# A hybrid layer on one Trainium2 core: the mixer's first loads, four fewer early units, and the routing stage's order

## The chip, the cores and the metric

The kernel runs on one core of one Trainium2 chip. The metric is device time in microseconds for one execution of the whole program, as the median of repeated runs. The engines are TensorE (PE, matmuls, with its weight loads shown as PEld), VectorE (DVE), ScalarE (ACT), GpSimd (POOL) and SyncE (SP, which here only issues DMAs). Each runs its own instruction stream in order, and they meet at semaphores.

## What is computed

One decoder layer on 2048 tokens of width 1024, all in float32:

```python
u = x*(1+scale1) + shift1                      # scale, shift, gates: silu(c) @ w_ada + b_ada
cb, cc, cx, q, k, v, ga, gb = split(u @ w_in)
y_a = (cb * causal_dwconv3(cc*cx)) @ w_a
y_b = stick_breaking_attention(q, k, v) @ w_b  # 8 heads of 64, no softmax
mix = (sigmoid(ga)*y_a + sigmoid(gb)*y_b) @ w_o
x = layer_norm(alpha*x + g1*mix)
u2 = x*(1+scale2) + shift2
# router: aff = sigmoid(u2 @ w_router); best group of 4 by its two best experts,
# top 2 of 16 experts inside it, gates normalized
x = layer_norm(alpha*x + g2*moe(u2))           # each expert: (silu(u@w_gate) * (u@w_up)) @ w_down
```

Float32 precision is reached with pairs: an operand is split into a rounded high part (`hi`, made by an ACT copy) and the rest (`lo`, a subtraction on DVE or POOL), and a product is three matmuls: hi*hi, hi*lo and lo*hi (`product`, line 92).

## The kernel before

The program is a row of stages. A stage is a block: every engine has a stream in it, and the next block begins on all engines when all streams of the last have ended.

**front** makes the first modulation rows, u and the projection to q, k and v, in 4 token blocks of 12 units each (48 units, `n` in the loops). A unit's result is evicted by ACT (hi, line 354) and DVE (lo, lines 412 and 416) into one of two stages and stored by SP (lines 226 to 231). Besides, front makes "halves": for a column block of `w_in` that the mixer needs, it loads 0.5 MB, splits it and stores hi and lo (1 MB) to DRAM. `FRONT_FILL` (line 436) is how many of them, 18, one at every second unit from 10 on (`FILL_AT`; load at line 210, store at line 216). At unit 36 SP also reloads u, 4 MB (line 246).

**mixer** has 8 heads of 16 query tiles (t = 0 to 15). For each tile: scores for two tiles ahead on PE (`scores`, lines 738 to 741), two sigmoids on ACT (851, 852), a scan on DVE (907), a product on POOL (700, `weigh`), transposes on PE (752), hi on ACT (870) and lo on DVE (915), then values on PE (771, 773). Between these PE fills in the projection to the convolution and gate columns: 14 units per head, 8 contraction steps each, cut over the slots by `fill_plan`. Units 0 to 13 belong to head 0, 14 to 27 to head 1; they are one token block, and later token blocks use the same 28 halves again. Unit n below 18 takes its halves from DRAM (`load_halves`, 553). Units 18 to 27 load the raw block (561), split it on ACT (843) and POOL (693), and SP keeps the result in DRAM (543). Scores need key block 0 (`k0`) for t below 4 and the rest of the keys (`k`, 1.5 MB, lines 575 and 582) from the second bank of t = 4 on, which PE works on in step t = 2. After each even tile DVE adds a modulation piece (`add_mod`, 964 and 967), 64 pieces of 0.25 MB in all; PE sums a head's pieces at its end (line 806). `k0` of head 0 is loaded through ACT's queue (835). SP's list starts with q, halves 0, q, v0, halves 1, k, mod 0, mod 1, v (lines 624 to 632).

**branch_outputs** makes the merged branches. **mix_norm_route** then does, for each of 16 token tiles t: `mix(t)`, 48 matmuls in 8 portions of 6 (PE, two PSUM buffers); `norm` on DVE (1519 to 1525); reciprocal deviation on POOL (1459 to 1463); the normalization on ACT (1402); `affine` on DVE (1531, 1533), which gives u2; scaling of x1 on POOL (1472, 1474); on PE the turn of u2 of tile t-2 (1300) inside step t; its copy out of PSUM on ACT (`rows_out`, 1381), then the logits on PE (1312) and a sigmoid on ACT (1390). ACT's order in step t is `rows_out(t-2)`, normalization of t, `high(t+3)`, `affinities(t-2)`. Tiles are grouped in sets; for a set DVE runs `choose` and `weigh` (1547 to 1589, some 27 small operations), PE ranks (1322, 1323), DVE runs `put` (1598 to 1603), and POOL scatters the records (1446, two per tile). At the end DVE makes the table of blocks (1624 to 1643). During this stage SP also loads expert 0's weights.

**experts** then reads the record of block 0 (POOL, 1709), gathers its rows (1719), turns them (PE, 1762), splits expert 0's gate and up weights (ACT 1829, DVE 1883, eight chunks each), and runs the blocks. **final_norm** ends it.

The order around the change is written out by hand:

```python
SETS = ((0, 4), (4, 8), (8, 12), (12, 14), (14, 16))
CHOOSE_AT = {5: 0, 9: 1, 13: 2, 16: 3, 17: 4}   # DVE step: set
RANK_AT = {7: 0, 11: 1, 15: 2, 17: 3, 18: 4}    # PE step: set (DVE's put too)
```

Of the kernel before, what the change touches and what calls it, by code (L numbers as in the profile page):

```python
# [435 lines left out]
FRONT_FILL = 18  # L436
# [18 lines left out]
def mixer(nc, used, keep, w_in, w_ada, u, u_in, u_saved, qk_hi, qk_lo, v_tok, halves, conv_t, gate_t, o_t, mod_rows):  # L455
# [49 lines left out]
    with ExitStack() as ctx:  # L505
# [32 lines left out]
        def _(sp):  # L538
# [91 lines left out]
            load_mod(0)  # L630
# [548 lines left out]
def mix_norm_route(nc, used, keep, stay, ahead, w_gate, w_up, w_down, m_t, x, mod_rows, ln1_g, ln1_b, w_router, b_router, acc, u2_rows, records):  # L1179
# [3 lines left out]
    SETS = ((0, 4), (4, 8), (8, 12), (12, 14), (14, 16))  # L1183
# [4 lines left out]
    CHOOSE_AT = {5: 0, 9: 1, 13: 2, 16: 3, 17: 4}  # L1188
    RANK_AT = {7: 0, 11: 1, 15: 2, 17: 3, 18: 4}
    with ExitStack() as ctx:  # L1190
        s = Scope(nc, ctx, "mix", used)
# [5 lines left out]
        y, x1t = s.sb("y", [P, D]), s.sb("x1t", [P, 2, D])  # L1197
# [88 lines left out]
        def _(pe):  # L1286
# [70 lines left out]
        def _(act):  # L1357
# [35 lines left out]
            for t in range(STEPS):  # L1393
# [20 lines left out]
        def _(pool):
# [34 lines left out]
            def scatter_at(step):  # L1449
                for at_step, g in RANK_AT.items():  # L1450
                    for t in range(*SETS[g]):
                        if step == min(at_step + 1 + t - SETS[g][0], max(at_step + 1, NT)):
                            scatter(t)

            for t in range(NT + 4):
                if t < NT:
                    past(pool, m["normed"], t)
                    pool.wait_ge(m["var_done"], t + 1)
                    pool.tensor_scalar(var[:], mv[:, 1:2], EPS, None, ALU.add).then_inc(m["var_step"], 1)
                    pool.wait_ge(m["var_step"], 2 * t + 1)  # L1460
                    pool.tensor_tensor(rstd[:], var[:], minus_half[:], ALU.pow).then_inc(m["var_step"], 1)
                    pool.wait_ge(m["var_step"], 2 * t + 2)
                    pool.tensor_scalar(offset[:], mv[:, 0:1], rstd[:], -1.0, ALU.mult, ALU.mult
                                       ).then_inc(m["rstd_done"], 1)
# [633 lines left out]
```

## Time and profile before

| What | Value |
|---|---|
| Median of 3 runs | 2816.57 us (2816.51 to 2819.57) |
| Profiled execution | 2813.91 us |
| Its span, first to last instruction | 2812.3 us |
| PE / DVE / ACT / POOL busy | 2507.2 / 1479.4 / 1114.9 / 816.4 us |
| Granted TensorE clock, mean | 0.949 |
| Halves loads in the mixer | 102 pairs of 512 KB |

The profile's page gives each engine's busy share in 40 slices. Views of the trace used below are the windows (busy time of each engine in a stretch, and PEclk, the granted share of full clock: 1.00 is 2.4 GHz and 0.50 is 1.2 GHz), the timeline (start, duration, engine, line, instruction and, in brackets, how long the engine had been idle before it and what released it), and the list of DMA issues with the median time to landing.

### The profile page before, as it was taken

What the parts mean: (1) busy time and instruction counts of PE and PEld (TensorE: products, weight loads), DVE (VectorE), ACT (ScalarE), POOL (GpSimd) and SP (SyncE); (2) the same over time, 40 slices, a digit from 0 to 9 for tenths busy, and PEclk for the clock granted to TensorE, in tenths of its full rate; (3) what the DMA queues carried; (4) which work ended last, traced back from release to release, by engine and by line L of the source; (5) the groups of instructions that cost most, each with busy time, mean ns of one, the idle gap of its engine ahead of it and who ended that gap; (6) DMA issues with size and microseconds to landing.
All of it is one profiled execution on the core that took longest, in us unless ns stands there. A gap on an engine that the chain in (4) does not pass through costs nothing. (4 is left out here: it accounts for less than half of the span.)

```text
span 2812.3 us, 36346 instructions
## 1 busy us (share of the span) xinstructions
PE 2507.2 (89%) x12521; PEld 2092.3 (74%) x12522; DVE 1479.4 (53%) x1898; ACT 1114.9 (40%) x1814; POOL 816.4 (29%) x703
## 2 busy tenths in 40 slices
PE   5999789999999999999968969983998999999970
PEld 4788578878888888888857758773887888888750
DVE  6122156666566656566632256765446544526636
ACT  2122244545454545454520012112456545536633
POOL 2111022442222222222301235456222222223236
PEclk9999899999999999999989989995999999999985
DMA  7699966766757574746456646423467655636735
GB/s 265 243 317 311 308 201 193 245 207 214 220 174 216 177 232 159 214 152 199 146 185 221 175 152 230 144 98 120 136 185 237 206 145 175 208 89 208 255 75 239
DMA packets 259931, 553.75 MB, mean 197 GB/s; under 512 B 23989, under 2 KB 93737, under 8 KB 259177
## 3 DMA queue, kind: packets, MB, share of 16 engines
q1 hardware_dynamic: 236904, 486.74, 52.4%
q0 software_dynamic: 15248, 46.62, 7.6%
q10 hardware_dynamic: 7664, 18.88, 1.7%
q8 instruction: 70, 1.15, 0.2%
q14 instruction: 45, 0.36, 0.0%
HBM read 399.14 MB, written 153.02 MB: 196 GB/s over the span
## 5 line engine op out<-in xcount | busy, mean ns | idle before, releaser
L92 PE MATMUL mx_acc<-u_u,mx_w_hi 128*128 128x512 f32 x1792 | 569.5, 399 | 0.9 <-DMA mx_w_lo<-halves 0.6
L700 POOL TENSOR_TENSOR mx_wt<-mx_wt,mx_rest 128x127 f32<-128x127 f32 (+15 forms) x128 | 271.5, 2121 | 764.7 <-DVE mx_rest L907 764.7
L92 PEld LDWEIGHTS mx_acc<-u_u,mx_w_hi 128*128 128x128 f32 x1792 | 325.0, 189 | 65.5 <-DMA mx_w_lo<-halves 1.9
L915 DVE TENSOR_TENSOR mx_wt_lo<-mx_p_t,mx_wt_hi 128x512 fp32r<-128x512 f32 (+2 forms) x320 | 192.3, 605 | 317.4 <-ACT mx_wt_hi L870 315.6
L92 PE MATMUL mx_acc<-u_u,mx_w_lo 128*128 128x512 f32 x896 | 351.7, 393 | 0.0
L870 ACT ACTIVATE mx_wt_hi<-mx_p_t 128x512 fp32r<-128x512 f32 (+2 forms) x320 | 171.0, 534 | 415.8 <-PE mx_p_t L752 358.5
L907 DVE TENSOR_TENSOR_SCAN mx_rest<-mx_rest,mx_zero 128x128 f32<-128x128 f32 (+15 forms) x128 | 312.1, 2438 | 11.4 <-ACT mx_wt L852 11.4
L92 PE MATMUL moe_p_gu<-moe_gu_hi,moe_x_hi 128*128 128x512 f32 x656 | 262.3, 400 | 15.1 <-DVE moe_gu_lo L1883 13.0
L92 PE MATMUL moe_p_gu<-moe_gu_hi,moe_x_lo 128*128 128x512 f32 x656 | 258.2, 394 | 0.0
L92 PE MATMUL moe_p_gu<-moe_gu_lo,moe_x_hi 128*128 128x512 f32 x656 | 258.0, 393 | 0.0
L851 ACT ACTIVATE mx_rest<-mx_p_z 128x512 f32<-128x512 f32 (+2 forms) x320 | 171.0, 534 | 96.3 <-PE mx_p_z L739 59.3
L92 PEld LDWEIGHTS mx_acc<-u_u,mx_w_lo 128*128 128x128 f32 x896 | 169.1, 189 | 38.5
L752 PE MATMUL mx_p_t<-keep_ident,mx_wt 128*128 128x128 f32 x1088 | 174.6, 276 | 25.8 <-POOL mx_wt L700 19.2
L752 PEld LDWEIGHTS mx_p_t<-keep_ident,mx_wt 128*128 128x128 f32 x1088 | 134.1, 141 | 80.9 <-POOL mx_wt L700 36.0
L852 ACT ACTIVATE mx_wt<-mx_p_z 128x512 f32<-128x512 f32 (+2 forms) x320 | 171.7, 536 | 0.0
L92 PE MATMUL fr_acc<-u_u,fr_w_hi 128*128 128x512 f32 x512 | 162.3, 399 | 6.5 <-DVE fr_stage L412 6.3
L1883 DVE TENSOR_TENSOR moe_gu_lo<-keep_stay,moe_gu_hi 128x1024 fp32r<-128x1024 f32 x128 | 146.8, 1219 | 28.4 <-ACT moe_gu_hi L1829 28.4
L1927 DVE TENSOR_TENSOR moe_h<-moe_p_gu,moe_act_g 128x256 f32<-128x256 f32 x82 | 31.0, 420 | 237.3 <-ACT moe_act_g L1860 237.3
L92 PEld LDWEIGHTS moe_p_gu<-moe_gu_hi,moe_x_hi 128*128 128x128 f32 x656 | 124.8, 190 | 41.2 <-DVE moe_gu_lo L1883 13.7
L738 PE MATMUL mx_p_z<-mx_k_hi,mx_q 128*128 128x512 f32 (+2 forms) x320 | 131.2, 410 | 19.4 <-DMA mx_k_lo<-qk_lo 19.4
L92 PEld LDWEIGHTS moe_p_gu<-moe_gu_hi,moe_x_lo 128*128 128x128 f32 x656 | 124.8, 190 | 27.1
L92 PEld LDWEIGHTS moe_p_gu<-moe_gu_lo,moe_x_hi 128*128 128x128 f32 x656 | 124.8, 190 | 25.2
(244 smaller groups left out, 5160.6 us busy)
## 6 DMA issues: line engine op xcount, KB each, us to landing
mx_w_hi<-halves SPq DMA_DIRECT2D x102, 512.0 KB, 3.9
mx_w_lo<-halves SPq DMA_DIRECT2D x102, 512.0 KB, 5.2
keep_stay<-in_w_gate SPq DMA_DIRECT2D x64, 512.0 KB, 4.3
keep_stay<-in_w_up SPq DMA_DIRECT2D x64, 512.0 KB, 5.2
keep_stay<-in_w_down SPq DMA_DIRECT2D x32, 1024.0 KB, 6.8
halves<-fr_ring SPq DMA_DIRECT2D x36, 512.0 KB, 6.5
u_saved<-u_u SPq DMA_DIRECT2D x4, 4096.0 KB, 19.5
mx_w_mod<-in_w_ada SPq DMA_DIRECT2D x64, 256.0 KB, 5.1
```

The lines of the kernel that those rows point to most:

```text
L92: mm = pe.matmul(out, a, b, start=first and n == 0, stop=last and n == len(pairs) - 1, skip_group_check=True)
L700: pool.tensor_tensor(wt[:, t % 2, 0:w - 1], wt[:, t % 2, 0:w - 1], rest[:, t % 2, 1:w], ALU.mult).then_inc(m["weights_done"], 1)
L738: pe.matmul(out, q, hi, start=True, stop=False, skip_group_check=True)
L752: mm = pe.transpose(p_t[:, n % TR, (j - 4 * r) * P:(j - 4 * r + 1) * P], wt[:, t % 2, j * P:(j + 1) * P], ident[:])
L851: act.activation(rest[:, t % 2, a:b], p_z[:, n % ZB, 0:b - a], ACT.Sigmoid, scale=-SCALE)
L852: act.activation(wt[:, t % 2, a:b], p_z[:, n % ZB, 0:b - a], ACT.Sigmoid, scale=SCALE).then_inc(m["z_used"], 1)
L870: act.activation(to, p_t[:, n % TR, 0:(k - j) * P].rearrange("p (j t) -> p j t", t=P), ACT.Copy).then_inc(m["hi_done"], 1)
L907: dve.tensor_tensor_scan(x[:, ::-1], x[:, ::-1], zero[:].to_broadcast([P, w]), 1.0, ALU.mult, ALU.max).then_inc(m["scan_done"], 1)
L915: dve.tensor_tensor(wt_lo[:, first:first + k - j], p_t[:, n % TR, 0:(k - j) * P].rearrange("p (j t) -> p j t", t=P), f32(wt_hi[:, first:fi ...
L1883: dve.tensor_tensor(lo, raw, f32(hi), ALU.subtract).then_inc(m["gu_lo_done"], 1)
L1927: dve.tensor_tensor(h[:, w], p_gu[:, 1, w], act_g[:, w], ALU.mult).then_inc(m["h_done"], 1)
```

## The change

- `FRONT_FILL` goes from 18 to 14. Front makes halves for head 0 only, and the mixer splits units 14 to 27.
- In the mixer `k0` of head 0 is issued by SP, first in its list; modulation piece 0 becomes fourth in the list (after `k0`, q and halves 0).
- Routing: the set (14, 16) becomes two sets of one tile; choices, ranks and puts get new steps, with `put` in a table of its own; PE turns after portion 0, ranks after portion 2 and does the logits after portion 3; ACT does `affinities(14)` after the normalization of 15; POOL's scatters are written out by step, some behind the x1 work.
- The table's last matmul uses the other half of the PSUM tile, and waits for the affinities.
- The first block's record and gather move from the experts stage to the end of the routing stage, on POOL. `y` of the routing stage and `x_raw` of the experts are one tile.
- `w_hi`, `w_lo` of the routing stage and `gu_hi`, `gu_lo` of the experts are one pair of tiles ("wide"). ACT makes all eight high chunks of expert 0 at the end of routing, DVE four low chunks; in the experts stage DVE makes two, then the low part of x, then the last two.
- In the experts stage PE turns x before its twelve transposes of zeros, POOL's memsets of the down weights come after gather 1, and SP waits for the first gather before it loads expert 1.

```diff
-FRONT_FILL = 18
+FRONT_FILL = UNITS_HEAD
@@ mixer, sync
+            load_k0(0)
             load_q(0)
             load_halves(0)
+            load_mod(0)
             load_q(1)
             load_v0(0)
             load_halves(1)
             load_k(0)
-            load_mod(0)
             load_mod(1)
@@ mixer, scalar
-            for half in range(2):
-                rows = slice(half * HD, (half + 1) * HD)
-                for dst, src in ((k0_hi, qk_hi), (k0_lo, qk_lo)):
-                    act.dma_start(f32(dst[rows, 0]), src[AW:AW + HD, 0:NB]).then_inc(k0_in[0], 16)
@@ mix_norm_route
-    SETS = ((0, 4), (4, 8), (8, 12), (12, 14), (14, 16))
+    SETS = ((0, 4), (4, 8), (8, 12), (12, 14), (14, 15), (15, 16))
-    CHOOSE_AT = {5: 0, 9: 1, 13: 2, 16: 3, 17: 4}
-    RANK_AT = {7: 0, 11: 1, 15: 2, 17: 3, 18: 4}
+    CHOOSE_AT = {5: 0, 9: 1, 13: 2, 14: 3, 15: 4, 16: 5}
+    RANK_AT = {7: 0, 11: 1, 15: 2, 16: 3, 17: 4, 18: 5}
+    PLACE_AT = {7: 0, 11: 1, 14: 2, 15: 3, 16: 4, 17: 5}
+    SCATTER_AT = {8: (0,), 9: (1,), 10: (2,), 11: (3,), 12: (4, 5), 13: (6, 7), 15: (10, 11)}
+    SCATTER_LATE = {14: (8, 9), 15: (12, 13, 14, 15)}
@@ mix_norm_route, tensor
-                        if k == 1:
+                        if k == 0:
                             turn(t - 2)
-                        if k == 5:
+                        if k == 2 and t in RANK_AT:
+                            rank(RANK_AT[t])
+                        if k == 3:
                             logits(t - 2)
-                        if k == 5 and t in RANK_AT:
-                            rank(RANK_AT[t])
...
-            pe.wait_ge(m["rank_used"], len(SETS))
-            pe.matmul(p_r[:, 1, 0:E], ones[:], seen[:, NT], start=True, stop=True).then_inc(m["ranked"], 1)
+            pe.wait_ge(m["aff_done"], len(SETS))
+            pe.matmul(p_r[:, 0, 0:E], ones[:], seen[:, NT], start=True, stop=True).then_inc(m["ranked"], 1)
@@ mix_norm_route, scalar
+                if t == NT - 1:
+                    affinities(NT - 2)
...
+            act.wait_ge(m["mix_done"], NT)
+            for k in range(KD):
+                if k % PIECE == 0:
+                    act.wait_ge(ahead["piece"][k // PIECE], 32)
+                act.activation(w_hi[:, k], gu_raw[:, k], ACT.Copy).then_inc(m["gu_hi_done"], 1)
@@ mix_norm_route, gpsimd
+            pool.wait_ge(m["row_set"], 1)
+            start = pool.value_load(block_row[0:1, 0:1], min_val=0, max_val=E * CAP)
+            pool.wait_ge(m["record_set"], 1)
             pool.wait_ge(m["scattered"], 32 * NT)
+            pool.dma_start(record[:, 4], records[bass.ds(start, P), :]).then_inc(ahead["record_in"], 16)
+            for i in range(UR):
+                pool.wait_ge(u2_stored[i], 16 * len(range(i, NT, UR)))
+            pool.wait_ge(m["normed"], NT)
+            pool.wait_ge(ahead["record_in"], 16)
+            pool.indirect_dma_start(out=first["x_raw"][:], out_offset=None, in_=u2_rows,
+                                    in_offset=bass.IndirectOffsetOnAxis(ap=record[:, 4, 0:1], axis=0)
+                                    ).then_inc(ahead["x_in"], 16)
@@ mix_norm_route, vector
+            for k in range(LO_AHEAD):        # LO_AHEAD = 4
+                dve.wait_ge(m["gu_hi_done"], k + 1)
+                dve.tensor_tensor(w_lo[:, k], gu_raw[:, k], f32(w_hi[:, k]), ALU.subtract).then_inc(m["gu_lo_done"], 1)
@@ experts
 sync:    +            sp.wait_ge(m["x_in"], 16)
 gpsimd:  -            load_record(0)
          -            gather_x(0)
 tensor:  +            turn_x(0)      (before the transposes of zeros, was behind them)
 vector:  -            split_gu(0, None)
          +            split_gu(0, 0, range(LO_AHEAD, LO_AHEAD + 2))
                       low_x(0)
          +            split_gu(0, 0, range(LO_AHEAD + 2, KD))
```

## Rows read from the trace of the kernel before

**Rows 1.** Windows: busy us (x) of PE, PEld, DVE, ACT, POOL; PEclk; DMA; GB/s

```profile
1890.00:1960.00 70.00, 27.82 (x126) 23.91 (x124) 41.24 (x117) 13.70 (x18) 39.95 (x36) 0.61 0.24 84
```

**Rows 2.** Timeline, front's end: start, us, engine, line, instruction [idle before <-releaser]

```profile
326.12 0.39 PE L92 MATMUL fr_acc<-fr_w_hi,u_u 128*128 128x512 f32 x1
...
329.57 0.60 ACT L354 ACTIVATE fr_stage<-fr_acc 128x512 fp32r<-128x512 f32 x1 [2.30 <-DMA v_tok<-fr_stage]
```

**Rows 3.** Timeline of PE and DVE, the mixer's start

```profile
345.89 0.44 PE L738 MATMUL mx_p_z<-mx_k_hi,mx_q 128*128 128x128 f32 x1 [19.38 <-DMA mx_k_lo<-qk_lo]
...
360.74 0.49 DVE L964 TENSOR_SCALAR mx_m_sum<-mx_w_mod,keep_csilu 128x512 f32<-128x512 f32 x1 [10.70 <-DMA mx_w_mod<-in_w_ada]
...
363.42 0.90 PE L752 MATMUL mx_p_t<-keep_ident,mx_wt 128*128 128x128 f32 x3 [6.69 <-POOL mx_wt L700]
...
366.36 1.16 PE L92 MATMUL mx_acc<-u_u,mx_w_hi 128*128 128x512 f32 x2
```

**Rows 4.** DMA issues, 335 to 375 us: KB each, median us to landing

```profile
mx_k_lo<-qk_lo SPq DMA_DIRECT2D x2, 384.0 KB, 13.1
```

**Rows 5.** Timeline of PE, line 806: ends of heads 0, 1, 2

```profile
490.93 1.00 PE L806 MATMUL mx_p_o<-keep_one,mx_m_sum 128*128 128x1 f32 x8
...
626.73 1.00 PE L806 MATMUL mx_p_o<-keep_one,mx_m_sum 128*128 128x1 f32 x8
...
758.97 1.00 PE L806 MATMUL mx_p_o<-keep_one,mx_m_sum 128*128 128x1 f32 x8
```

**Rows 6.** Timeline of PE, ACT and DVE, a regular routing step

```profile
1796.36 1.03 PE L1300 MATMUL mix_p_t<-keep_ident,mix_u 128*128 128x128 f32 x8
...
1800.10 1.06 ACT L1381 ACTIVATE mix_u2t<-mix_p_t 128x512 f32<-128x512 f32 x2
...
1802.69 1.85 PE L1312 MATMUL mix_p_r<-mix_wr,mix_u2t 128*128 128x16 f32 x16
...
1809.98 1.03 PE L1300 MATMUL mix_p_t<-keep_ident,mix_u 128*128 128x128 f32 x8
...
1807.46 1.28 DVE L1519 SCALAR_TENSOR_TENSOR mix_y<-keep_stay,mix_p_mix 128x512 f32<-128x512 f32 x2 [2.38 <-PE mix_p_mix L92]
```

**Rows 7.** Timeline of PE and DVE, routing step 11, behind a choice

```profile
1836.08 3.59 PE L1312 MATMUL mix_p_r<-mix_wr,mix_u2t 128*128 128x16 f32 x16 [5.99 <-ACT mix_u2t L1381]
...
1844.34 0.40 PE L92 MATMUL mix_p_mix<-mix_w_hi,mix_a_hi 128*128 128x512 f32 x1
...
1845.23 1.28 DVE L1519 SCALAR_TENSOR_TENSOR mix_y<-keep_stay,mix_p_mix 128x512 f32<-128x512 f32 x2 [5.31 <-PE mix_p_mix L92]
```

**Rows 8.** Timeline of POOL and DVE, the routing stage's end

```profile
1902.79 2.37 POOL L1474 TENSOR_TENSOR mix_x1t<-mix_x1t,mix_ln_b 128x1024 f32<-128x1024 f32 x1
...
1907.47 1.28 DVE L1519 SCALAR_TENSOR_TENSOR mix_y<-keep_stay,mix_p_mix 128x512 f32<-128x512 f32 x2 [6.96 <-PE mix_p_mix L92]
...
1917.78 2.42 DVE L1549 TENSOR_TENSOR mix_pairs<-mix_sel 128x128 f32<-128x128 f32 x1
...
1926.92 0.18 DVE L1547 TENSOR_TENSOR mix_sel<-mix_aff,mix_br 128x32 f32<-128x32 f32 x1
...
1933.66 0.22 DVE L1598 TENSOR_TENSOR mix_picked<-mix_chosen,mix_p_r 128x64 f32<-128x64 f32 x1 [0.24 <-issue]
...
1943.37 0.20 DVE L1643 CAST keep_block_row<-mix_p_t 1x54 int32<-1x54 f32 x1 [0.46 <-PE mix_p_t L1354]
```

**Rows 9.** Timeline of POOL and PE, the first expert block

```profile
1947.11 0.11 POOL L1723 MEMSET moe_record<- 128x10 uint32 x1 [6.92 <-POOLq L1190]
...
1967.27 0.79 PE L92 MATMUL moe_p_gu<-moe_gu_hi,moe_x_hi 128*128 128x512 f32 x1 [2.09 <-DVE moe_x_lo L1917]
```

**Rows 10.** Timeline of PE, routing step 2

```profile
1694.98 1.93 PE L1312 MATMUL mix_p_r<-mix_wr,mix_u2t 128*128 128x16 f32 x16 [2.67 <-ACT mix_u2t L1381]
```

**Rows 11.** DMA issues of the whole run, POOL's loads

```profile
moe_record<-records POOLq DMA_DIRECT2D x46, 1.0 KB, 3.1
moe_x_raw<-u_rows,moe_record POOLq DMA_INDIRECT x45, 5.1
```

More of the change, by code:

```diff
@@ L1447, in scatter @@
                                             ).then_inc(m["scattered"], 16)
[L1449 to L1464, printed above, removed]
+            pool.memset(record[:], 0).then_inc(m["record_set"], 1)
+            for t in range(NT):
+                past(pool, m["normed"], t)
+                pool.wait_ge(m["var_done"], t + 1)
+                pool.tensor_scalar(var[:], mv[:, 1:2], EPS, None, ALU.add).then_inc(m["var_step"], 1)
+                pool.wait_ge(m["var_step"], 2 * t + 1)
+                pool.tensor_tensor(rstd[:], var[:], minus_half[:], ALU.pow).then_inc(m["var_step"], 1)
+                pool.wait_ge(m["var_step"], 2 * t + 2)
+                pool.tensor_scalar(offset[:], mv[:, 0:1], rstd[:], -1.0, ALU.mult, ALU.mult
+                                   ).then_inc(m["rstd_done"], 1)
                 if t == 0:
@@ L1651, in experts @@
         gu_raw, dn_raw = expert_raw(stay)
-        gu_hi, gu_lo = s.sb("gu_hi", [P, KD, 2, FF], F32R), s.sb("gu_lo", [P, KD, 2, FF], F32R)
+        gu_hi, gu_lo = (w[:].rearrange("p k (g f) -> p k g f", g=2) for w in wide)
         dn_hi, dn_lo = s.sb("dn_hi", [P, KF, D], F32R), s.sb("dn_lo", [P, KF, D], F32R)
-        x_raw = s.sb("x_raw", [P, D])
+        x_raw, record = first["x_raw"], first["record"]
         x_hi, x_lo = s.sb("x_hi", [P, KD, P], F32R), s.sb("x_lo", [P, KD, P], F32R)
@@ L1875, in _, with split_gu @@
             dve.sem_inc(m["y_free"], 3)
+            dve.sem_inc(m["gu_lo_done"], LO_AHEAD)
             dve.sem_inc(m["dn_lo_done"], KF)
-            def split_gu(e, done):
-                for c in range(KD):
+            def split_gu(e, done, chunks=range(KD)):
+                for c in chunks:
                     raw, hi, lo = chunk(c)
@@ L2055, in hybrid_layer @@
             "table": s.sb("table", [P, 4, E], I32), "block_row": s.sb("block_row", [P, ROWS], I32),
-            "csilu": s.sb("csilu", [P, KD]), "one": s.sb("one", [P, 1]), "spare": s.sb("spare", [P, 24]),
+            "csilu": s.sb("csilu", [P, KD]), "one": s.sb("one", [P, 1]), "spare": s.sb("spare", [P, 8]),
+            "record": s.sb("record", [P, 5, 2], U32),
             "marks": {n: s.sem(f"mark_{n}") for n in ("sp", "act", "pool", "pe", "dve")},
         }
-        ahead = {"w_o": [s.sem(f"w_o{k}") for k in range(KD)], "piece": [s.sem(f"piece{i}") for i in range(PIECES)]}
+        ahead = {"w_o": [s.sem(f"w_o{k}") for k in range(KD)], "piece": [s.sem(f"piece{i}") for i in range(PIECES)],
+                 "record_in": s.sem("record_in"), "x_in": s.sem("x_in")}
         with ExitStack() as uctx:
@@ L2069, in hybrid_layer @@
         branch_outputs(nc, used, keep, stay, ahead, conv_t, o_t, gate_t, w_a, w_b, w_o, m_t)
-        mix_norm_route(nc, used, keep, stay, ahead, w_gate, w_up, w_down, m_t, x, mod_rows, ln1_g, ln1_b, w_router, b_router,
+        wide = tuple(s.sb(n, [P, KD, D], F32R) for n in ("wide_hi", "wide_lo"))
+        first = {"record": keep["record"], "x_raw": s.sb("x_raw", [P, D])}
+        mix_norm_route(nc, used, keep, stay, ahead, wide, first, w_gate, w_up, w_down, m_t, x, mod_rows, ln1_g, ln1_b, w_router, b_router,
                        acc, u2_rows, records)
@@ L2074, in hybrid_layer @@
             ln_g, ln_b = ls.sb("g", [P, D]), ls.sb("b", [P, D])
-            experts(nc, used, keep, stay, ahead, w_gate, w_up, w_down, mod_rows, ln2_g, ln2_b, u2_rows, records, acc, ln_g, ln_b)
+            experts(nc, used, keep, stay, ahead, wide, first, w_gate, w_up, w_down, mod_rows, ln2_g, ln2_b, u2_rows, records, acc, ln_g, ln_b)
             final_norm(nc, used, acc, ln_g, ln_b, out)
```

63 lines of the change are left out of this document (33 added, 30 removed).

## The prediction

> **What bounds the kernel now.** I read the windows by stage first. TensorE (PE) is nearly always busy, except where two stages meet and in the routing stage; in the 70 us at that stage's end it is busy for 27.8 at a granted clock of 0.61 [rows 1]. So a change pays only where it shortens a PE gap, and it costs wherever PE is made to wait. Next I read the timeline of the three places that the diff touches, with the idle time in brackets.
>
> Front into mixer: PE's last matmul starts at 326.12, but the last eviction of its results waits for an older store and starts at 329.57 [rows 2]. The mixer's first matmul comes at 345.89, after 19.4 us. Ten us later VectorE (DVE) stands 10.7 us for modulation piece 0, then PE stands 6.7 us for weights that come out of DVE and GpSimd (POOL) [rows 3].
>
> Routing: in a regular step PE turns tile t-2 after two of the eight portions and does its logits after six; ScalarE (ACT) finishes the copy that the logits need at 1801.16, 1.5 us ahead of PE [rows 6]. Where DVE chooses experts, that copy is late, since it sits on ACT behind the next tile's normalization, and PE stands 6 us [rows 7]. After the last mix DVE is the bound: normalization, two choices, the table [rows 8]. Then comes the gather of the first block [rows 9].
>
> **Part 1, front tail: -3.0 us.** The last four fills (halves made at units 38 to 44) go. Each was a 0.5 MB load and a 1 MB store on SP's queue. With that queue light the last eviction can start when PE ends (326.5) and not at 329.57: -3.0 [rows 2]. Ends: 0 if the u reload alone fills the queue, -5 if the last store lands sooner too.
>
> **Part 2, mixer start: -5 us.** Key block 0, q, halves 0 and modulation piece 0 are now in front. The 10.7 us wait for the piece, and PE's 6.7 behind it, vanish. What is late next is the rest of k, which the scores of t = 4 need right after the turn of t = 2. It is issued in this window with a median of 13.1 us to landing [rows 4], the last one 10 us after the mixer's start, so it is there at about 358.5, and 1.2 us later now that 0.26 MB of the piece goes ahead of it. Old PE passed that point at 365.8, just before the fill at 366.36 [rows 3]; new PE would, on the old clock face, at 359.7: -6.1. PE then still has waited some 5 us, so its clock is low for a few us as it is now, which takes 1 back. Ends: -3 (k later), -9.5 (k in time: 6.7 of wait and 3 of low clock saved).
>
> The key loads move from ACT's queue to SP's, past q, halves and v: 4 issues, 2.4 us later for all behind them. The Trainium skill (DMA: Bandwidth & Descriptors, "Issuing engines are not separate DMA queues") says that transfers of all engines interleave on the same 16 DMA engines and that a second issuer saves only issue time. By it this move costs 2.4 us of issue and wins no bandwidth, and the 3 us by which the first matmul might come earlier are not won in the end, since k still decides; this agrees with how I took it.
>
> **Part 3, four more units split in head 1: +1.5 us.** Head 1, with ten such units, lasts 135.8 us, head 2 with none 132.2 [rows 5]: 0.36 us each, so 1.4, and a little for units 14 to 17, which fall on short steps where POOL's 2.4 us subtraction stands before the next weights. Ends: 0 and +4.
>
> **Part 4, logits after the fourth portion, turn after the first: +14.9 us.** A portion is about 1.36 us (13.62 us from turn to turn, less turn and logits, over eight) [rows 6]. New turn: one portion earlier, 1795.0 on the row's clock; logits reached 0.9 + 3 x 1.36 later, at 1800.0. The copy is ready at 1801.16, because it waits on ACT behind the normalization of t-1, which hangs on the end of mix(t-1) and not on the turn. So PE waits 1.1 us where it waited for nothing. DVE waits 2.4 us for the mix of such a step [rows 6], so it isn't the bound and the step gets longer by all of it. Steps 3, 4, 5, 8, 9, 12 and 13: 7 x 1.1 = 7.7. Steps 6, 10 and 14 lie ahead of a choice that decides anyway. In steps 7 and 11 PE resumes at the same time as before, but with 24 matmuls to go instead of 12 and the rank already done. The clock stays low to 1844.3 [rows 7]: from the end of the logits at 1839.6 that is 11 matmuls of 0.43, then 13 of 0.23 (a portion's 1.36 over six), so 1847.3 and not 1845.2: +2.1 and, where the low clock lasts longer, +2.4; together 4.4. Step 2 waits for its logits as well: 12 matmuls more behind the wait, +2.8. Ends for all: +5 (no wait in regular steps) and +27 (each wait brings low clock).
>
> **Part 5, the last sets and the handover: -5.2 us.** Three choices of (12,13), 14 and 15 replace two. The first now runs before norm(15): DVE is held by POOL's x1 work to 1905.2, choice and gates take 6, so norm(15) starts at 1911.3 and not 1907.47: +3.8 [rows 8]. After that DVE has two choices as before, 6.7 us each from 1926.92 to 1933.66 [rows 8], once with POOL's two 2.5 us operations in its way as before; POOL's scatters of 10 and 11 only shift them. Table ready: 1947.6 instead of 1943.57, +4.0. Handover, before: 1943.57 to the first expert matmul at 1967.27 is 23.7, of it 3.5 to the next block's first instruction [rows 9]. After: 1.2 to read the row, 3.1 for the record (median to landing), 1.3 to issue the gather [rows 11], then the same 3.5, x there by then (5.1 from issue), turn 2.0 and the twelve zero transposes 3.0, now behind the turn: about 14.5, so -9.2. The weight splits, 9 us of DVE, hide behind it. Net -5.2; ends -9 and +2. The memsets of the down weights (7.1 us of POOL) are now behind gather 1 and end about when PE wants them, 13 us after its first matmul.
>
> That POOL holds DVE is read from a 0.29 us operation that took 2.42 [rows 8]. The Trainium skill (GPSIMD Engine Reference, Specifications) says that POOL shares its SBUF interface with VectorE and contends with VectorE instructions in a two-port mode or with two SBUF inputs. By it choice 14 is held for the 5 us of x1(15); if it were not, the sum would be 4.6 lower.
>
> **Sum:** -3.0 - 5.0 + 1.5 + 14.9 - 5.2 = +3.2. The profiled execution is 2813.91 (span 2812.3), so 2817.1; it lies 2.7 below the median of 2816.57, to which I add the same: 2819.8.
>
> **Rivals.**
> - A, the fourth portion costs nothing: copies are there, or the DVE backlog swallows the waits. For it: the first steps' waits hang on DVE. Against: the copy's end is 4.8 us behind the old turn in each regular step. Then 14.9 falls away: -11.7, 2805. Chance 0.12.
> - B, each new 1.1 us wait also brings low clock, on the slow side. Place: the regular routing steps. Step 2's wait of 2.7 us before the logits at 1694.98 had a short stretch of low clock behind it [rows 10]. Nine matmuls at 0.43 instead of 0.23 are 1.8; 1.8 x 7 = +12.6, so +15.8, 2832. It decides from where PE's share of a step is too small to hold the clock. Against: 1.1 is less than half of that wait, and PE is busy for 13.6 of 14.7 us. Chance 0.12.
> - C, the handover gives nothing: DVE's extra 4 us grow, as the scatters push POOL's x1 into the choices, and gather and block end queue up. Price +5.2: +8.4, 2825. Chance 0.12.
> - D, k comes in time, and the whole wait and low clock in head 0 go: -4.5 more, -1.3, 2815. Chance 0.14.
> - My forecast: 0.50, by itself 2815 to 2826.
>
> **How the numbers follow.** A measurement tells 0.2%, 5.6 us, from no change. Faster: A and a little of D, 0.14. Slower: B, most of C, and a fifth of my own case, 0.33. Same: 0.53. The range leaves out half of A and half of B: 2807 to 2832.
>
> **What would show it.** Right: the first mixer matmul some 5 to 7 us earlier; DVE without the wait for the piece and PE waiting for k instead; a bracket of about 1.1 us before the logits in regular routing steps, with 14.7 us from turn to turn; the table about 19 us later than before relative to the stage's start; some 14.5 us from table to first expert matmul. Wrong if regular steps still last 13.6, if k is no wait, or if the handover stays near 24.

## The result and the profile after the change

| | before | after |
|---|---|---|
| Median | 2816.57 us | 2830.55 us (2829.43 to 2843.11) |
| Ratio to before | | 1.0056, 95% interval 1.0042 to 1.0070 |
| Profiled execution, its span | 2813.91, 2812.3 us | 2829.43, 2826.7 us |
| Granted TensorE clock, mean | 0.949 | 0.948 |

The change makes the kernel slower by 0.56%, some 16 us. The forecast was 2819.8 us and no change; the time lies at the upper end of its range, where rival B stood (2832).

I compared the two traces at marks that both have. Times are from each kernel's own start; "first mix" is PE's first `mix_p_mix` matmul, "norm of 14" is DVE's first operation on the mix of tile 14, and "table" is DVE's cast of the block row.

| Mark or stretch | before | after | difference | forecast |
|---|---|---|---|---|
| First mixer matmul | 345.89 | 336.46 | -9.4 | -6 |
| End of head 0 | 490.93 | 480.11 | -10.8 | -8.0 |
| Head 1 | 135.80 | 140.24 | +4.4 | +1.5 |
| End of the mixer's last head | 1417.35 | 1411.08 | -6.3 | -6.5 |
| Mixer's end to first mix | 233.17 | 235.29 | +2.1 | 0 |
| First mix to norm of tile 14 | 242.06 | 266.46 | +24.4 | +14.9 |
| Norm of 14 to norm of 15 | 14.89 | 18.77 | +3.9 | +3.8 |
| Norm of 15 to table | 35.90 | 29.83 | -6.1 | +0.2 |
| Table to first expert matmul | 23.90 | 16.13 | -7.8 | -9.2 |
| First expert matmul to the end | 845.0 | 849.1 | +4.1 | 0 |

The stretch between mixer and first mix is untouched code; in the other kernels below it lasted between 229.9 and 236.7 us with no pattern, so its 2.1 us are scatter. The mixer's start scatters too: in the five kernels here with the old front and the old load order the first mixer matmul comes at 343.7 to 347.2 us and head 0 ends at 488.1 to 493.4, so differences to the one trace of before are good to some 3 us there.

**The mixer's start.** This timeline of after (start, duration, engine, line, instruction, and in brackets the idle time before it and its releaser) answers to [rows 2, 3].

```profile
324.02 0.39 PE L93 MATMUL fr_acc<-fr_w_hi,u_u 128*128 128x512 f32 x1
324.45 0.60 ACT L355 ACTIVATE fr_stage<-fr_acc 128x512 fp32r<-128x512 f32 x1 [4.84 <-PE fr_acc L93]
336.46 0.44 PE L740 MATMUL mx_p_z<-mx_k_hi,mx_q 128*128 128x128 f32 x1 [12.04 <-DMA mx_q<-qk_lo]
352.95 0.47 PE L740 MATMUL mx_p_z<-mx_k_hi,mx_q 128*128 128x128 f32 x1 [4.66 <-DMA mx_k_lo<-qk_lo]
353.47 0.75 DVE L964 SCALAR_TENSOR_TENSOR mx_m_sum<-mx_w_mod,keep_csilu,mx_m_sum 128x512 f32<-128x512 f32 x1 [2.48 <-DMA mx_w_mod<-in_w_ada]
```

The last eviction now waits for PE and not for a store. PE's 6.7 us behind DVE's wait are gone; the rest of k is late next, for 4.66 us, and DVE waits 2.5 us for a later piece, off the path.

**Head 1.** PE's timeline, its head ends and two waits in between that before hadn't (its longest in these tiles was 0.86 us).

```profile
480.11 1.00 PE L808 MATMUL mx_p_o<-keep_one,mx_m_sum 128*128 128x1 f32 x8
485.59 0.44 PE L754 MATMUL mx_p_t<-keep_ident,mx_wt 128*128 128x128 f32 x2 [1.78 <-POOL mx_wt L702]
508.01 0.65 PE L754 MATMUL mx_p_t<-keep_ident,mx_wt 128*128 128x128 f32 x4 [2.64 <-POOL mx_wt L702]
620.35 1.00 PE L808 MATMUL mx_p_o<-keep_one,mx_m_sum 128*128 128x1 f32 x8
```

POOL splits the weights of units 14 to 17 there, and its product for the attention comes late: 4.4 us for both waits, about what head 1 lost.

**Routing.** Two regular steps of after against [rows 6]: the logits with their wait, some of the matmuls behind them, the next turn.

```profile
1739.34 1.96 PE L1314 MATMUL mix_p_r<-mix_wr,mix_u2t 128*128 128x16 f32 x16 [1.09 <-ACT mix_u2t L1383]
...
1741.94 0.45 PE L93 MATMUL mix_p_mix<-keep_wide_hi,mix_a_hi 128*128 128x512 f32 x1
1742.19 0.63 PE L93 MATMUL mix_p_mix<-keep_wide_lo,mix_a_hi 128*128 128x512 f32 x1
1742.62 0.63 PE L93 MATMUL mix_p_mix<-keep_wide_hi,mix_a_lo 128*128 128x512 f32 x1
1743.04 0.63 PE L93 MATMUL mix_p_mix<-keep_wide_hi,mix_a_hi 128*128 128x512 f32 x1
...
1745.18 0.57 PE L93 MATMUL mix_p_mix<-keep_wide_hi,mix_a_lo 128*128 128x512 f32 x1
1745.59 0.39 PE L93 MATMUL mix_p_mix<-keep_wide_hi,mix_a_hi 128*128 128x512 f32 x1
...
1790.26 1.03 PE L1302 MATMUL mix_p_t<-keep_ident,mix_u 128*128 128x128 f32 x8
1793.26 1.24 ACT L1404 ACTIVATE mix_x1t<-keep_x_raw,mix_offset,mix_rstd 128x1024 f32<-128x1024 f32 x1 [16.19 <-POOL mix_offset L1466]
1795.36 1.06 ACT L1383 ACTIVATE mix_u2t<-mix_p_t 128x512 f32<-128x512 f32 x2
1796.47 1.96 PE L1314 MATMUL mix_p_r<-mix_wr,mix_u2t 128*128 128x16 f32 x16 [1.09 <-ACT mix_u2t L1383]
1798.28 0.49 PE L93 MATMUL mix_p_mix<-keep_wide_hi,mix_a_hi 128*128 128x512 f32 x1
...
1805.23 1.03 PE L1302 MATMUL mix_p_t<-keep_ident,mix_u 128*128 128x128 f32 x8
```

The wait is the forecast's, 1.09 us, and for its reason: the turn ends at 1791.3 and the copy starts at 1795.36, behind the normalization. Behind the second wait the matmuls go on at 0.23 us and the step lasts 14.97 us. Behind the first they fall to 0.43 us (the lower of the clock's two levels, 1.2 GHz) for eight matmuls, and that step lasts 16.6. Of the seven regular steps three lose 1.3 us against the 13.6 of before, and four lose 2.95.

**The end of routing and the first blocks**, against [rows 8, 9].

```profile
1912.83 1.28 DVE L1535 SCALAR_TENSOR_TENSOR keep_x_raw<-keep_stay,mix_p_mix 128x512 f32<-128x512 f32 x2
1931.60 1.28 DVE L1535 SCALAR_TENSOR_TENSOR keep_x_raw<-keep_stay,mix_p_mix 128x512 f32<-128x512 f32 x2
1959.42 0.96 POOL L1455 DMA_INDIRECT records<-mix_meta,mix_dest  x1 [0.30 <-issue]
1961.43 0.20 DVE L1659 CAST keep_block_row<-mix_p_t 1x54 int32<-1x54 f32 x1 [0.46 <-PE mix_p_t L1356]
1963.41 0.60 POOL L1484 DMA_DIRECT2D keep_record<-records  x1 [3.04 <-DMA records<-mix_meta,mix_dest]
1966.28 1.02 POOL L1489 DMA_INDIRECT keep_x_raw<-u_rows,keep_record  x1 [2.27 <-DMA keep_record<-records]
1972.59 1.94 PE L1779 MATMUL moe_p_x<-keep_ident,keep_x_raw 128*128 128x128 f32 x8 [11.20 <-PEq L1190]
1976.48 0.59 POOL L1729 DMA_DIRECT2D keep_record<-records  x1 [1.34 <-issue]
1977.56 0.53 PE L93 MATMUL moe_p_gu<-keep_wide_hi,moe_x_hi 128*128 128x512 f32 x1 [0.47 <-DVE moe_x_lo L1934]
1982.72 1.02 POOL L1739 DMA_INDIRECT keep_x_raw<-u_rows,keep_record  x1 [5.66 <-DMA keep_record<-records]
1990.13 1.10 PE L1779 MATMUL moe_p_x<-keep_ident,keep_x_raw 128*128 128x128 f32 x8 [1.36 <-DMA keep_x_raw<-u_rows,keep_record]
1992.54 0.49 PE L93 MATMUL moe_p_y<-moe_dn_hi,moe_h_hi 128*128 128x512 f32 x1 [1.30 <-DVE moe_y L1927]
```

POOL asks for the first record as soon as the last scatter has landed (3.04 us), and no longer waits for the change of blocks. But the record of the second block takes 5.66 us where the first took 2.27, and PE waits 1.36 and 1.30 us for what hangs on it.

### The profile page after: what moved, and what is told of

Its sections match the earlier page's. It is cut to its first block and busy times, and to the rows that moved or that the text cites. A ratio compares the mean times of both kernels' runs of the same rounds, so it can differ in the third digit from the quotient of the medians.

```text
span 2826.7 us, 36389 instructions
## 1 busy us (share of the span) xinstructions
PE 2519.8 (89%) x12525; PEld 2098.2 (74%) x12526; DVE 1486.5 (53%) x1924; ACT 1114.9 (39%) x1815; POOL 826.1 (29%) x707
## 5 line engine op out<-in xcount | busy, mean ns | idle before, releaser
L93 PE MATMUL moe_p_gu<-keep_wide_hi,moe_x_hi 128*128 128x512 f32 x656 | 262.3, 400 | 13.5 <-DVE keep_wide_lo L1900 13.0
L93 PE MATMUL moe_p_gu<-keep_wide_hi,moe_x_lo 128*128 128x512 f32 x656 | 257.9, 393 | 0.0
L93 PE MATMUL moe_p_gu<-keep_wide_lo,moe_x_hi 128*128 128x512 f32 x656 | 257.3, 392 | 0.0
L1900 DVE TENSOR_TENSOR keep_wide_lo<-keep_stay,keep_wide_hi 128x1024 fp32r<-128x1024 f32 x124 | 142.3, 1220 | 30.0 <-ACT keep_wide_hi L1846 22.3
L93 PEld LDWEIGHTS moe_p_gu<-keep_wide_hi,moe_x_hi 128*128 128x128 f32 x656 | 124.7, 190 | 39.4 <-DVE keep_wide_lo L1900 13.7
L93 PEld LDWEIGHTS moe_p_gu<-keep_wide_hi,moe_x_lo 128*128 128x128 f32 x656 | 124.3, 189 | 27.0
L93 PEld LDWEIGHTS moe_p_gu<-keep_wide_lo,moe_x_hi 128*128 128x128 f32 x656 | 125.0, 190 | 25.1
```

The source lines that it names most:

```text
L93: mm = pe.matmul(out, a, b, start=first and n == 0, stop=last and n == len(pairs) - 1, skip_group_check=True)
L1900: dve.tensor_tensor(lo, raw, f32(hi), ALU.subtract).then_inc(m["gu_lo_done"], 1)
```

## Experiments

Theory 1: the loss is Part 4, each wait before the logits and the low clock behind it. Its rival: the waits cost only themselves, and the rest comes from the sets, the scatters, or the early place of turn and logits as such. Second question: what Parts 1 to 3 and 5 are worth, and where the handover's gain goes. All ratios are to the kernel before.

### Part 4 undone, and Part 4 alone

`undo4`, on the changed kernel (`only4` is the reverse, on the kernel before):

```diff
-                        if k == 0:
+                        if k == 1:
                             turn(t - 2)
-                        if k == 2 and t in RANK_AT:
-                            rank(RANK_AT[t])
-                        if k == 3:
+                        if k == 5:
                             logits(t - 2)
+                        if k == 5 and t in RANK_AT:
+                            rank(RANK_AT[t])
```

> The changed kernel with Part 4 alone undone: turn after the second portion, logits and rank after the sixth, all else as changed. Theory 1 (each new 1.1 us wait before the logits also brings low clock behind it, so the regular steps last 15 to 16.8 us): the norm of tile 14 falls from 266.5 us after the first mix to about 242 (before: 242.1), the regular steps are 13.62 us again, and the time falls by about 24 us, to about 2806, which is faster than before. Rival (the waits cost only their own 1.1 us, and the rest of the loss in the stage comes from elsewhere, the new sets or the scatters written out by step): the time falls by 11 to 15 us only, and some regular steps stay over 14 us.

> The kernel before with Part 4 alone: turn after the first portion, rank after the third, logits after the fourth. Theory 1: slower than before by about 24 us (2841), with waits of 1.1 us before the logits in steps 3 to 5, 8, 9, 12 and 13, a granted clock in the routing stage lower than before, and matmuls 0.43 us apart behind the waits. Rival (waits at their own price): slower by 11 to 15 us, clock as before.

`undo4`: 2808.10 us, ratio 0.9963 (0.9951 to 0.9975), faster than before. `only4`: 2843.56 us, 1.0095 (1.0077 to 1.0113). Norm of 14 stands 242.55 us behind the first mix in `undo4` (266.46 in after, 242.06 before) and 265.17 in `only4`. Part 4 costs 23 to 24 us in either setting by the traces, and 26 to 27 by the times. The forecast's terms for it were 14.9, the rival's 11 to 15. The windows of the 235 us behind the first mix (columns: busy us of PE, PEclk, DMA share, GB/s), first `undo4`:

```profile
1652.34:1887.34 235.00, 215.21 (x1037) 0.92 0.48 165
```

after:

```profile
1646.37:1881.37 235.00, 203.96 (x925) 0.88 0.46 155
```

PE does 112 instructions fewer in the same time, at a lower granted clock (0.87 in `only4`). Over the whole stage, 49 `mix_p_mix` matmuls of `undo4` and 93 of after start 0.38 to 0.47 us behind the last one, instead of 0.23: 44 more at some 0.2 us each, about 9 us of low clock. Theory 1 holds.

### Is it the wait or the place?

`copy_first`, on the changed kernel, ACT alone; turn and logits stay where the change put them:

```diff
-                if t < NT:
-                    rows_out(t - 2)
                 if t == NT - 1:
                     affinities(NT - 3)
-                    rows_out(NT - 2)
+                if t < NT:
+                    rows_out(t - 1)
                 if t < NT:
                     act.wait_ge(m["rstd_done"], t + 1)
```

> The changed kernel with one more edit, on ACT: in its step t it copies the turn of tile t-1 ahead of the normalization of tile t, where it copied the turn of t-2. The turn after the first portion and the logits after the fourth stay. Theory 1 (the wait is ACT's order, and the low clock is the wait's): the 1.1 us brackets before the logits are gone, the regular steps last about 13.6 us, the 6 us stall behind a choice shrinks too; the norm of tile 14 comes at 242 us after the first mix or earlier (down to 225 if the choices' stalls go), so the time falls by 24 to 40 us, to 2791 to 2806. Rival (the early place of turn and logits itself lowers the clock, since narrow matmuls stand closer together): the steps stay above 15 us though the waits are gone, and the time falls by less than 12 us.

2789.21 us, ratio 0.9895 (0.9876 to 0.9914). A step in its timeline:

```profile
1808.26 1.03 PE L1302 MATMUL mix_p_t<-keep_ident,mix_u 128*128 128x128 f32 x8
1809.33 1.09 ACT L1383 ACTIVATE mix_u2t<-mix_p_t 128x512 f32<-128x512 f32 x2 [9.86 <-PE mix_p_t L1302]
1815.18 1.85 PE L1314 MATMUL mix_p_r<-mix_wr,mix_u2t 128*128 128x16 f32 x16
1818.42 1.25 ACT L1403 ACTIVATE mix_x1t<-keep_x_raw,mix_offset,mix_rstd 128x1024 f32<-128x1024 f32 x1 [8.01 <-POOL mix_offset L1465]
```

```profile
1647.33:1882.33 235.00, 222.89 (x1128) 0.96 0.49 169
```

The copy stands right behind the turn, nobody waits, regular steps last 13.6 us, and 21 matmuls in the stage are at low clock. The early places themselves cost nothing. The 6 us stalls behind a choice [rows 7] have gone too: norm of 14 comes at 223.96 us.

`logits_k4`, on the changed kernel:

```diff
-                        if k == 3:
+                        if k == 4:
                             logits(t - 2)
```

> The changed kernel with the logits one portion later, after the fifth; the turn after the first portion and the rank after the third stay. The copy is ready at 1801.16 on the old clock face, and PE comes to the logits at 1801.3, so the regular steps should have no wait or one under 0.3 us. Theory 1 (low clock comes of the wait): regular steps 13.6 to 13.9 us, norm of tile 14 at about 245 us after the first mix, time about 18 to 22 us below the changed kernel, 2809 to 2813. Rival (the low clock comes of the places of turn and logits, or of the new sets): regular steps stay over 15 us, time falls by less than 10.

2808.09 us, ratio 0.9969 (0.9956 to 0.9981), as `undo4`; regular steps of 13.62 us with no wait, norm of 14 at 243.14 us, and a granted clock of 0.92 over 235 us. One portion more ahead of the logits removes both the wait and the clock's loss.

`logits_k2`, on the changed kernel:

```diff
-                        if k == 3:
+                        if k == 2:
                             logits(t - 2)
```

> The changed kernel with the logits one portion earlier still, after the third (ahead of them the rank, where there is one). The wait of the regular steps should be 1.1 + 1.36 = 2.5 us. Theory (the step gets longer by the wait and by low clock behind it): regular steps of 17 to 19 us where the changed kernel has 15 to 16.8, and 10 to 25 us more than it, 2840 to 2856. Rival (PE's wait is compensated since DVE, which needs 11 to 14 us a step, is not the bound and the step's end is set by the mix alone): less than 8 us more.

2855.54 us, ratio 1.0143 (1.0126 to 1.0160). One of its steps, and its window:

```profile
1829.76 1.96 PE L1314 MATMUL mix_p_r<-mix_wr,mix_u2t 128*128 128x16 f32 x16 [2.44 <-ACT mix_u2t L1383]
1841.46 1.03 PE L1302 MATMUL mix_p_t<-keep_ident,mix_u 128*128 128x128 f32 x8
```

```profile
1650.68:1885.68 235.00, 198.74 (x850) 0.84 0.44 149
```

Waits of 2.44 us make regular steps of 17.9 and 19.5 us: the wait itself, and 1.8 to 3.5 us beyond it, now in every step. So at 0, 1.1 and 2.4 us of wait a regular step loses 0, 2.2 (mean) and some 5 us.

`b_copy`, the diff of `copy_first` on the kernel before:

> The kernel before with the ACT edit alone: the copy of the turn of t-1 stands ahead of the normalization of t. Turn and logits stay at their old places (after the second and the sixth portion), so no place has moved. Theory 1 (what counts is whether PE waits behind ACT's order): the 6.0 us waits before the logits behind a choice go, regular steps stay at 13.6 us, the stage to the norm of tile 14 shortens from 242 us to 220 to 228, the time falls by 14 to 22 us, to 2796 to 2804. Rival (the copy needs the early turn to be out of the normalization's way: with the turn after the second portion ACT holds the normalization, DVE's affine comes 2 us late in each step): the regular steps last 14 to 15.5 us and the time falls by less than 8.

2792.97 us, ratio 0.9905 (0.9892 to 0.9918). Norm of 14 at 221.84 us, no wait before any logits up to tile 13. With the turn after the second portion DVE has 1.5 to 2.0 us of slack in a regular step instead of 2.4, so the copy does push the normalization a little, but not enough to matter. The early places of Part 4 buy nothing that the copy's order doesn't: norm of 14 comes at 223.96 us with them.

### Parts 1 to 3

`b_fill14`, on the kernel before:

```diff
-FRONT_FILL = 18
+FRONT_FILL = 14
```

> The kernel before with FRONT_FILL 14 alone. Theory (Parts 1 and 3 as the trace of after shows them): the front ends about 3 us earlier, head 1 lasts 140 to 141 us instead of 136 with two new waits for POOL's product in its first tiles, and the net is 0 to +2 us: the same time. Rival (the front's early end comes from the key block's loads leaving ACT, not from the fills): the front ends as before, head 1 costs its 4.5 us, net +4 to +5.

2817.59 us, ratio 0.9993 (0.9984 to 1.0002). In its timeline:

```profile
325.85 0.60 ACT L354 ACTIVATE fr_stage<-fr_acc 128x512 fp32r<-128x512 f32 x1 [4.84 <-PE fr_acc L92]
340.28 0.45 PE L738 MATMUL mx_p_z<-mx_k_hi,mx_q 128*128 128x128 f32 x1 [14.46 <-DMA mx_k_lo<-qk_lo]
628.69 1.00 PE L806 MATMUL mx_p_o<-keep_one,mx_m_sum 128*128 128x1 f32 x8
```

The front's tail goes and the mixer starts 5.6 us earlier; head 1 lasts 143.85 us, 8 us more than before and 3 more than I expected of this run, and eats it. In the ten kernels here with 14 fills head 1 lasts 140.2 to 144.2 us, in the seven with 18 it lasts 135.8 to 136.3.

`b_loads`, on the kernel before, with the key block's loads taken off ACT:

```diff
+            load_k0(0)
             load_q(0)
             load_halves(0)
+            load_mod(0)
             load_q(1)
             load_v0(0)
             load_halves(1)
             load_k(0)
-            load_mod(0)
...
```

> The kernel before with the mixer's load order alone: key block 0 on SP's queue and first, modulation piece 0 fourth. Theory (Part 2): DVE's 10.7 us wait for the piece goes, PE waits 4 to 5 us for k instead of 6.7 for the weights; head 0 ends 5 to 7 us earlier than before, and the time falls by as much, to 2810 to 2813. Rival (the gain in head 0 needs the light queue of FRONT_FILL 14, since k lands behind the front's last stores): head 0 ends less than 3 us earlier.

2811.68 us, ratio 0.9976 (0.9967 to 0.9986); head 0 ends at 485.35, 5.6 us earlier (2.7 to 8.0 against the five kernels with the old order). PE waits 5.57 us for k. Part 2 works by itself, as forecast.

`copy_fill18`, on `copy_first`:

```diff
-FRONT_FILL = UNITS_HEAD
+FRONT_FILL = 18
```

> The changed kernel with the ACT edit and FRONT_FILL 18. Theory (head 1's extra 4.4 us are the four units split in the mixer, the front's tail of 3 us is the four fills): head 1 back at 136 us, first mixer matmul 2 to 4 us later, net 0 to -3 us against the kernel with the ACT edit alone, so 2786 to 2790. Rival (head 1's loss comes from the new load order, its halves landing late): head 1 stays at 140, and the time is 2 to 4 us above it.

2790.01 us, ratio 0.9897 (0.9884 to 0.9911), as `copy_first`. First mixer matmul at 342.60, head 1 back at 135.76. Parts 1 and 3 cancel, and head 1's loss comes with the split units of Part 3, not with the load order.

### Part 5

`part5_only`, the changed kernel with `undo4`'s edit, `FRONT_FILL = 18` and the old load order, so the kernel before with Part 5 alone:

> The kernel before with Part 5 alone (sets, scatters by step, record and gather moved, shared weight tiles). Theory (from first mix to the first expert matmul it saves 9 to 10 us, and the experts stage gives 3 of them back): faster than before by 5 to 8 us, 2809 to 2812. Rival (the parts of the change don't add up: the gain of the changed kernel with Part 4 undone, 10.4 us, comes mostly of Parts 1 to 3, 7.4 us by their own runs): faster by 2 to 4 us.

2808.48 us, ratio 0.9977 (0.9968 to 0.9986). From first mix to first expert matmul it takes 306.9 us (before 316.75), and the first three blocks last 55.0 us (52.1).

`b_scatter`, the kernel before with POOL's scatters at the new steps and the third `put` one step earlier:

```diff
+    PLACE_AT = {7: 0, 11: 1, 14: 2, 17: 3, 18: 4}
+    SCATTER_AT = {8: (0,), 9: (1,), 10: (2,), 11: (3,), 12: (4, 5), 13: (6, 7), 15: (10, 11)}
+    SCATTER_LATE = {14: (8, 9), 15: (12, 13, 14, 15)}
...
```

> The kernel before with POOL's scatters at the changed kernel's steps (and the third put one step earlier), so that at most four tiles are scattered behind the last x1 work where it was eight. Theory (the old stage ends with POOL's row of 16 scatters at 1.27 us, and the next block's start hangs on it and not on the table): from the norm of tile 15 to the first expert matmul 59 us shrink to 49 to 54, the time falls by 5 to 10 us, to 2808 to 2813. Rival (the forecast's: the table, and then record, gather and block end, set the handover): from table to first expert matmul stays as it is, 24 to 29, and so does the time, within 2 us of before.

2815.83 us, ratio 1.0002 (0.9993 to 1.0011): my theory fell. In its timeline:

```profile
1926.48 0.96 POOL L1449 DMA_INDIRECT records<-mix_meta,mix_dest  x1 [0.31 <-issue]
1929.91 0.96 POOL L1449 DMA_INDIRECT records<-mix_meta,mix_dest  x1 [2.46 <-DVE mix_dest L1603]
1933.60 0.20 DVE L1643 CAST keep_block_row<-mix_p_t 1x54 int32<-1x54 f32 x1 [0.46 <-PE mix_p_t L1357]
1933.71 0.96 POOL L1449 DMA_INDIRECT records<-mix_meta,mix_dest  x1 [0.30 <-issue]
1943.05 0.60 POOL L1709 DMA_DIRECT2D moe_record<-records  x1 [1.14 <-issue]
```

POOL is done early and then waits 2.46 us for the last put; the four scatters of tiles 14 and 15 stand behind that in any case, and the record load 9.3 us behind the last of them (9.6 before). In the six kernels with the old handover this stretch is 9.1 to 9.9 us, while the record load stands 3.9 to 10.8 us behind the table: it hangs on the last scatter. What the change shortens is that stretch: 4.0 us in after.

`a_oldsets` and `c_oldsets`, the changed kernel and `copy_first` with tiles 14 and 15 in one set again:

```diff
-    SETS = ((0, 4), (4, 8), (8, 12), (12, 14), (14, 15), (15, 16))
-    CHOOSE_AT = {5: 0, 9: 1, 13: 2, 14: 3, 15: 4, 16: 5}
-    RANK_AT = {7: 0, 11: 1, 15: 2, 16: 3, 17: 4, 18: 5}
-    PLACE_AT = {7: 0, 11: 1, 14: 2, 15: 3, 16: 4, 17: 5}
+    SETS = ((0, 4), (4, 8), (8, 12), (12, 14), (14, 16))
+    CHOOSE_AT = {5: 0, 9: 1, 13: 2, 15: 3, 16: 4}
+    RANK_AT = {7: 0, 11: 1, 15: 2, 17: 3, 18: 4}
+    PLACE_AT = {7: 0, 11: 1, 14: 2, 16: 3, 17: 4}
```

> The changed kernel with its last two one-tile sets joined to one again (choices after the affine of 15 and behind it, as before), all else as changed. Theory (the third choice between the norms of 14 and 15 costs 3.8 us at norm 15 and DVE is bound from there): norm 15 comes 4 us earlier after norm 14, the last put comes somewhat earlier too, and the time falls by 2 to 8 us. Rival (splitting the sets pays, since it takes one tile less through the last choice and lets scatters start earlier): the time rises by 1 to 5 us.

> The changed kernel with the copy ahead of the normalization on ACT and the two last sets joined. With the copy first DVE is the bound, and the norm of 15 stood 18.6 us behind that of 14 (7.9 us in the kernel before with the same ACT edit). Theory: the joined sets give back 6 to 10 us of DVE time there, so the time falls to 2779 to 2784. Rival (scatters or the round trip between PE and DVE set the end): less than 3 us, 2786 to 2790.

2839.06 us, 1.0078 (1.0065 to 1.0092), and 2792.80 us, 0.9922 (0.9909 to 0.9935). My theory fell in both, and both came out above the rival's range too: slower than with the split sets, though the intervals of the pairs overlap. The traces agree with the sign. Norm of 15 does come earlier (8.9 us in `c_oldsets`, 1.2 in `a_oldsets`), but the last put now covers two tiles, and from the table to the first expert matmul it takes 21.6 us in `a_oldsets`, where after takes 16.1:

```profile
1965.78 0.20 DVE L1659 CAST keep_block_row<-mix_p_t 1x54 int32<-1x54 f32 x1 [0.47 <-PE mix_p_t L1356]
1973.37 0.59 POOL L1484 DMA_DIRECT2D keep_record<-records  x1 [2.02 <-DMA records<-mix_meta,mix_dest]
```

The record load comes 7.6 us behind the table; in after it is 2.0. From first mix to first expert matmul the split is worth 5.3 us in the changed kernel and 2.4 with the copy first.

`copy_latesp` and `a_latesp`, `copy_first` and the changed kernel with SP waiting for the second gather:

```diff
         @block.sync
         def _(sp):
-            sp.wait_ge(m["x_in"], 16)
+            sp.wait_ge(m["x_in"], 32)
```

> The changed kernel with the copy ahead of the normalization, and SP waiting for the second gather, not the first, before it loads expert 1's weights. Theory (in the first expert block the record of block 1 takes 5.7 us instead of 2.3 because four 1 MB pieces were issued just before it, and the second turn and the first down product wait for that): these two waits, 1.4 and 1.3 us, go, the blocks follow each other after 17.7 us and not 19.4, and the time falls by 1 to 3 us. Rival (the record is late for the block switch's own reasons): the waits stay, same time.

> The changed kernel with SP waiting for the second gather before it loads expert 1's weights, nothing else. Theory (these loads stood in the way of the record and gather of block 1, and the first two blocks lose by it): first to third turn of the experts stage 34 us instead of 36.9, time 3 to 5 us below the changed kernel, 2824 to 2827. Rival (it paid only where the routing stage ended early, on the kernel with the ACT edit): within 1.5 us of the changed kernel.

2782.37 us, 0.9881 (0.9867 to 0.9896), and 2826.98 us, 1.0042 (1.0029 to 1.0056): each 0.14% below its base, with intervals that overlap. The trace of `copy_latesp` shows what happens:

```profile
1936.09 0.59 POOL L1728 DMA_DIRECT2D keep_record<-records  x1 [1.33 <-issue]
1939.51 1.01 POOL L1738 DMA_INDIRECT keep_x_raw<-u_rows,keep_record  x1 [2.84 <-DMA keep_record<-records]
1944.04 0.40 SPq L122 DMA_DIRECT2D keep_stay<-in_w_gate  x1
1948.19 1.03 PE L1778 MATMUL moe_p_x<-keep_ident,keep_x_raw 128*128 128x128 f32 x8
```

The record takes 2.84 us and not 5.66, and the second turn has no wait. Three blocks last 51.8 us instead of 56.5 in `copy_first`, and 52.5 instead of 54.6 in the changed kernel. That the late loads pay rests on the traces; the times alone don't show it. By its median `copy_latesp` is the fastest kernel here, 1.2% below before.

## Why the prediction was wrong, point by point

- **Front tail (-3.0) and head 1 (+1.5)**: right in sum by luck, since both terms were too small. `b_fill14` starts the mixer 5.6 us earlier (3.4 to 6.9 against the five kernels with the old front) and gives it back in head 1, which lasts 8.1 us longer there and 4.4 in after; together -2.0 by the ratio (interval -4.5 to +0.6), forecast -1.5. In head 1 I took the mean price of a split unit; the four added ones stand in the first tiles, and there they make PE wait 1.8 and 2.6 us. I had named that place and given it almost nothing.
- **Mixer start (-5)**: held. `b_loads` gives -6.8 by the ratio (-9.3 to -3.9). DVE's wait is gone, and PE waits for k, 4.66 us where I had written some 5. Rival D (k in time) fell.
- **Logits and turn (+14.9)**: the step that failed. Its terms can be set beside the intervals from norm to norm, after less `undo4`. Step 2: forecast 2.8, measured 2.8. Steps 7 and 11: 4.4, measured 5.2. The seven regular steps: 7.7, measured 15.7 (1.28, 2.93, 2.95, 1.33, 2.95, 1.32, 2.96). Steps 6, 10 and 14: 0, measured 0. The wait itself was right to 0.03 us, though a step with it costs 1.3 and not 1.1 even where the clock holds. What I set at nothing is the low clock that stands behind four of the seven waits, 1.6 us each. Rival A, no wait, fell. Rival B had this mechanism and its unit price (1.8), but took it as all or nothing at 0.12. My argument against it, "1.1 is less than half of that wait, and PE is busy for 13.6 of 14.7 us", leaned on one row of a lone wait [rows 10]; it said nothing on a wait that comes back every 15 us.
- **Sets and handover (-5.2)**: right in sum by two errors. Norm of 15 is 3.9 us later as said. The rest of the way to the first expert matmul is 13.8 us shorter and not 9.0. The chain runs through the last scatter, not through the table, and I measured from the table. In the one profiled execution of before the table stood 35.9 us behind the norm of 15, where in `b_loads`, `b_fill14` and `b_scatter` it is 30.8 to 31.3; these kernels then take 27.8 to 29.0 us from table to first matmul, not 23.9, and the sum of both is 58.6 to 59.8 us in all four. So the 23.9 us that I worked from were too few by 4 to 5. Against this stand 2.5 to 2.9 us in the first three blocks, where expert 1's loads now meet the record of the second block. The late loads give them back. I had costed the moved gather, but not what it was moved next to. (The other 1.6 us of the last line of the table of marks aren't placed; from first expert matmul to the end it takes 843.9 to 848.0 us in the kernels with the old handover.) Rival C fell.
- **The sum**: the parts run alone give 0.9993 x 0.9976 x 0.9977 x 1.0095 = 1.0041, against 1.0056 for the whole, within their intervals. The times show no interaction between the parts, though one of up to some 0.4% would be hidden in these intervals; the term of Part 4 is the one with the wrong size.
- **The chances**: faster 0.14, same 0.53, slower 0.33. With a term whose own ends I had put at +5 and +27, taking the lower half on the strength of one row was too sure; the measured 24 is near the upper end.

What stays open: why three of the seven waits have no low clock behind them, though they are of the same length to 0.03 us. Which ones these are isn't fixed: in after they are those of steps 3, 8 and 12, in `only4` of 4, 8 and 13, and in `a_oldsets`, with waits as long, it is step 12 alone. Filling the wait with other PE work, which would separate idle time from the rest, wasn't tried.

## What to carry to other kernels

When a consumer's wait is moved, ask which instruction on the producer's engine stands ahead of the result, and whether the order there can be turned: here one moved copy on ACT was worth some 45 us on the changed kernel (1.0056 to 0.9895) and 27 on the one before (0.9905), where moving the consumer cost 24 to 27. A wait of PE in a loop has two prices, its length and the clock behind it; here a regular step lost twice the length in the mean, with waits of 1.1 us and of 2.4. When a stretch is shortened, measure from the event that the next stage really hangs on, and look at what its transfers then fall together with.

## What the runs showed of the hardware

- A 1.1 us gap of PE that recurs each 15 to 17 us of otherwise full work can lower the granted clock: behind four of seven such gaps in after (six of seven in `a_oldsets`, all seven with the 2.4 us gaps of `logits_k2`) some eight matmuls start 0.43 us apart and not 0.23, and the 235 us of the stage are granted 0.88 (0.92 without the gaps, 0.84 with gaps of 2.4 us, 0.96 with the longer stalls gone too).
- POOL waited 5.66 us for the record's load of 1 KB in after, where SP issued eight loads of weights from 1972.75 to 1980.32 around it, and 2.27 and 2.84 us (the first record of after, the second of `copy_latesp`) where SP issued none until the record was there. Under the late loads of `copy_latesp` it is the third record that takes 5.52 us, and there PE doesn't wait for it.
